# Sample attention of a decoder step: half of the page loads issued from GpSimd's queue

## What is computed

```
past = cache_kv_l[page_table].reshape(B, past_len, 4, N_KV, HEAD_DIM)     # B = 8, past_len = 2048
seq  = concatenate([past, rows, zeros])                                   # rows: the new tokens
kc, vc, ksb, vsb = branch_keys(seq, pe, w1, b1, w2)      # compressed keys; keys and values of blocks of 64
...
o_cmp = softmax(q kc) vc                                 # compressed branch; it also scores the blocks
kg, vg = ksb[top_k(score)], vsb[top_k(score)]            # 16 of 33 blocks of 64 tokens are selected
o_sel = softmax(q kg) vg
o_win = softmax(q kw) vw                                 # the last 512 tokens, from a window buffer
o = gates[0] * o_cmp + gates[1] * o_sel + gates[2] * o_win
```

## Time and profile before

| | |
|---|---|
| median of 3 runs | 1530.45 us (1529.3 to 1533.97) |
| the profiled execution | 1531.58 us, of which the span of the trace is 1529.9 us |
| mean granted TensorE clock | 0.992 of full speed |
| TensorE busy | 1434.4 us, 94% of the span |
| GpSimd busy | 480.1 us, 31% |
| sample attention loop | from about 1336 us to about 1512 us of the span |
| DMA moved in the whole span | 158.38 MB, mean 104 GB/s |

### The profile page before, as it was taken

How to read it: one execution, slowest core, us unless ns; L and a number is a source line. 1 busy time by engine, 2 the same in 40 slices (tenths; PEclk the granted TensorE clock), 3 DMA queues, 4 the chain that set the end, 5 groups by cost and what they waited for, 6 DMA issues and landing times.

```text
span 1529.9 us, 23043 instructions
## 1 busy us (share of the span) xinstructions
PE 1434.4 (94%) x8098; PEld 910.8 (60%) x8098; DVE 818.3 (53%) x1663; ACT 476.0 (31%) x1063; POOL 480.1 (31%) x449
## 2 busy tenths in 40 slices
PE   2999999999999999999999999999988889988886
PEld 2666666666666666777444444877755554455543
DVE  1578887888888888710112311132367774454443
ACT  1243343334434333222100000111355552064552
POOL 0855556566665555411100000000056562000000
PEclk9999999999999999999999999999999999999998
DMA  6543332333333312533510333114000004537870
GB/s 183 137 122 115 91 106 87 93 104 97 95 98 98 96 32 67 190 110 96 228 68 0 115 114 123 50 58 163 28 1 1 2 1 133 184 111 243 256 236 9
DMA packets 139549, 158.38 MB, mean 104 GB/s; under 512 B 16226, under 2 KB 103525, under 8 KB 139237
## 3 DMA queue, kind: packets, MB, share of 16 engines
q1 hardware_dynamic: 134162, 150.07, 31.5%
q10 hardware_dynamic: 5272, 6.83, 1.5%
HBM read 150.18 MB, written 16.38 MB: 109 GB/s over the span
## 4 chain that ended last, share of the span: by engine, by line
PE 84%; SPq 4%; DVE 3%; POOL 3%; issue 2%; ACTq 2%; DMA 2%; ACT 1%; DVEq 0%
PE bank L1354 25%; PE bank L1377 15%; PE bank L1531 8%; PE bank L1466 7%; PE bank L1493 5%; PE bank L1365 4%; PE bank L1693 4%; POOL arena L679 3%; PE bank L1639 2%; SPq L546 2%; PE bank L1670 2%; SPq L548 2%; PE bank L1654 2%; DMA arena<-in_cache_kv_dram 2%; DVE arena L1154 2%
## 5 line engine op out<-in xcount | busy, mean ns | idle before, releaser
L1014 DVE SCALAR_TENSOR_TENSOR arena<-arena 128x512 f32<-128x512 f32 x464 | 424.3, 988 | 0.0
L1354 PE MATMUL bank<-arena 128*128 128x288 f32 x1536 | 381.0, 408 | 0.9 <-DVE arena L981 0.9
L1354 PEld LDWEIGHTS bank<-arena 128*128 128x128 f32 x1536 | 292.0, 191 | 86.5 <-issue 8.3
L1377 PE MATMUL bank<-arena 128*128 128x508 f32 x512 | 239.8, 615 | 0.0
L1377 PEld LDWEIGHTS bank<-arena 128*128 128x128 f32 x512 | 93.3, 190 | 109.8 <-issue 109.8
L613 POOL TENSOR_TENSOR arena<-arena 128x248 f32<-128x248 f32 x128 | 134.1, 1082 | 1.3
L1531 PE MATMUL bank<-arena 128*128 128x288 f32 x512 | 127.0, 407 | 0.6 <-PE bank L1531 0.6
L398 DVE SCALAR_TENSOR_TENSOR arena<-arena,bank 128x512 f32<-128x512 f32 (+1 forms) x20 | 13.6, 680 | 209.8 <-PE bank L1466 160.8
L679 POOL TENSOR_SCALAR arena<-arena 128x128 f32<-128x128 f32 (+3 forms) x96 | 100.3, 1055 | 71.8 <-DVE arena L1162 71.8
L1531 PEld LDWEIGHTS bank<-arena 128*128 128x128 f32 x512 | 96.2, 190 | 27.3 <-issue 1.5
L1466 PE MATMUL bank<-arena 128*128 128x512 f32 x256 | 110.4, 592 | 0.0
(11 more groups left out here) (254 smaller groups left out, 1585.7 us busy)
## 6 DMA issues: line engine op xcount, KB each, us to landing
arena<-in_cache_kv_dram SPq DMA_DIRECT2D x256, 128.0 KB, 3.4
arena<-in_cache_kv_dram SPq DMA_DIRECT2D x128, 256.0 KB, 3.2
arena<-in_conv_w_in_dram SPq DMA_DIRECT2D x48, 512.0 KB, 4.2
arena<-in_nsa_w_in_dram SPq DMA_DIRECT2D x56, 256.0 KB, 4.7
arena<-in_conv_w_out_dram SPq DMA_DIRECT2D x16, 512.0 KB, 4.8
arena<-in_cache_win_dram SPq DMA_DIRECT2D x8, 1024.0 KB, 7.1
out_dram<-in_cache_win_dram SPq DMA_DIRECT2D x1, 8064.0 KB
arena<-in_x_prompt_dram SPq DMA_DIRECT2D x2, 2048.0 KB, 9.4
```

The costliest lines, as they stand in the source:

```text
L1014: ch.mark(dve.scalar_tensor_tensor(part, src, w, part, ALU.mult, ALU.add))
L1354: last = pe.matmul(bank[pair + h][:, 0:HALF], wi[:, n % WSLOT, k], xT[:, k, h * HALF:(h + 1) * HALF], start=k == 0, stop=k == KT - 1)
L1377: last = pe.matmul(out, wc[:, s, j, h * STEPS + k], x4[:, h, :, j:j + NC], start=(k == 0 and h == 0 and j == 0), stop=(k == STEPS - 1 and ...
```

## The change

The pages of buffers n = 2 and 3 are loaded from GpSimd's queue. SyncE keeps the windows and the buffers n = 0 and 1. The waits on `e_pv` and the completion semaphores are the same as before. GpSimd's new `load_pages` is the same function as SyncE's; for b = 0 its transfers stand ahead of the preparation of `vpair`, for b = 1 and later behind it.

```
+            def load_pages(b, n):
+                slot = (b % 2) * 4 + n
+                for i in range(4):
+                    pg = pool.value_load(pages[0:1, b * NPG + 4 * n + i:b * NPG + 4 * n + i + 1], min_val=0,
+                                         max_val=cache_kv.shape[1] - 1)
+                    pool.dma_start(kv[slot][:, i], cache_kv[0, bass.ds(pg, 1), :, 2:4].rearrange("o t s g d -> (o t) (s g d)")
+                                   ).then_inc(kv_in[slot], 16)
+
             pool.wait_ge(o_ev, KT)
+            for n in (2, 3):
+                load_pages(0, n)
             ch.link(pool.memset(vpair, 0.0))
             ch.link(pool.tensor_copy(vpair[0:64, :, HD:P], ...))
             pool.tensor_copy(vpair[64:128, :, 0:HD], ...).then_inc(staged, 1)
+            for n in (2, 3):
+                load_pages(1, n)
+            for b in range(2, NB):
+                for n in (2, 3):
+                    pool.wait_ge(e_pv, OUTS * (b - 2) + 3 + n)
+                    load_pages(b, n)
```

More of the change, by code:

```diff
@@ L558, in _ @@
             sp.dma_start(offs2, ln_b[1:2, :].broadcast_to([P, DM])).then_inc(s_ln, 16)
-            for n in range(4):
+            for n in range(2):
                 load_pages(0, n)
             load_window(1)
-            for n in range(4):
+            for n in range(2):
                 load_pages(1, n)
```

## The result

Slower: the median went from 1530.45 to 1541.66 us (1540.7 to 1545.52, five runs), a ratio of 1.0075 with a 95% interval of 1.0054 to 1.0096. I had said 1520.9.

What follows compares the result with a forecast made beforehand. The loop of freed buffer, SyncE's one-by-one page issue and landing was taken as the bound. A turn of 18.9 + 1.0 = 19.9 us against 21.51, six times, saves 9.6: from 1530.45 to 1520.9 us, range 1511 to 1545.

Steps and rivals of the forecast that it cites:

- What bounds the kernel: Sample attention loop: freed buffer, SyncE's page issues one after another, landing; better loading could give at most 21.7 us.
- SyncE's loop over eight pages: Sample attention loop: 11.8 us from buffer 0 freed to keys 2, 7.13 to weigh 2's end, 18.9 a turn.
- GpSimd's page: GpSimd's queue in the loop: register work 0.77 us plus issue 0.53 like a memset; its loop of 17.5 stays hidden.
- p: GpSimd's time per page in the loop, bounded between 0.77 and 2.63 us, taken as 1.30.
- Rival A: GpSimd's queue becomes the bound: each page costs it more than 1.87 us, slower, 1544 to 1562; chance 0.22.
- Rival C: VectorE keeps GpSimd from writing descriptors: 1.8 us a page, a turn of 21.0, time 1527; chance 0.06.
- The landing of GpSimd's pages: GpSimd's loop: 3.2 us from issue to landing; 0.4 more for its slower first byte would still be hidden.
- The two queues now overlap: GpSimd's pages beside SyncE's pages 5 to 8: SyncE's eighth lands 0.8 to 1.8 us later, 1.0 taken, 19.9 a turn.
- Rival B: The DMA engines are the bound: eighth page late by 2.0 to 2.6 us, time 1527 to 1530, no change; chance 0.13.
- The clock adds about 2 either way: TensorE after a 2 us wait at keys 2: a stretch at the lower clock may follow, or none; about 2 us.
- No cost ahead of the loop: Before the loop: GpSimd's first 8 pages take at most 21 us ahead of vpair, first read some 80 later.
- windows for nothing: Windows go out after weigh 0, 4.6 us before buffer 0 frees, landing in 7.3 with 10.5 to spare: no cost.

Runs made afterwards that it cites:

- Numbers ahead, on one queue: Kernel before, SyncE reading the page numbers of buffers 0 and 1 before waiting for buffer 0, issuing all sixteen pages: 1512.93 us, ratio 0.9891.
- half the bytes: Page loads bring only the keys, 128 KB of 256: changed kernel 1515.02 us, ratio 0.9899; kernel before 1520.95 us, ratio 0.9941.
- the last experiment: Changed kernel with SyncE's page numbers read ahead, plus the window issued after weigh 1 instead of weigh 0: 1510.53 us, ratio 0.9869.
- GpSimd held back: Changed kernel, GpSimd starting on a sequence's pages only when SyncE has issued its eight, from b = 2 on: 1543.27 us, ratio 1.01.
- the kernel with numbers ahead: Changed kernel, both queues, SyncE reading its eight page numbers before it waits for buffer 0: 1525.9 us, ratio 0.9981.
- swapped buffers: Changed kernel with the buffers exchanged, GpSimd loading 0 and 1, SyncE 2 and 3: 1552.41 us, ratio 1.0132.
- The filler: Changed kernel with 24 spare TensorE transposes ahead of the wait at keys 2, from b = 2 on: 1534.9 us, ratio 1.0031.
- buffers dealt in turn: Changed kernel with GpSimd loading buffers 1 and 3, SyncE 0 and 2: 1535.35 us, ratio 1.0029.

## Why the prediction was wrong

**What bounds the kernel: right.** The loop over freed buffer, issues and landing sets the turn. Numbers ahead, on one queue, and half the bytes both shortened it and the turn followed; with the waits nearly gone, the last experiment came to 17.99 us.

**SyncE's loop over eight pages: right as a term.** 11.8 us from freeing to keys 2 without the overlap was measured as 11.8 to 12.1 with GpSimd held back.

**GpSimd's page: right in kind, and cheaper.** p is 1.16 us, I took 1.30. Rival A is out: its eighth page of b = 4 was there at 1422.93 + 3.5 = 1426.4, and keys 4 came at 1432.60. Rival C is out too: the pages follow each other by 1.15 to 1.17 us whatever VectorE does, but for one gap of 1.45 in b = 3 and one in b = 6, which stand at the same pages in the shorter turns of the kernel with numbers ahead. The Trainium skill (SBUF — State Buffer, SBUF: two separate sides) names fast copies within SBUF as what locks GpSimd out of writing descriptors; VectorE's frequent copies here come from PSUM, and the even intervals agree.

**The landing of GpSimd's pages: right where they are alone.** A first page of buffer 0, with nothing beside it, lands in 2.9 to 3.3 us from GpSimd's queue (swapped buffers, mean of six 3.1) and in 2.4 to 2.9 from SyncE's (changed kernel, mean 2.6). The Trainium skill (DMA: Bandwidth & Descriptors, Latency and other measured facts) has about 0.4 us between the first bytes of the two kinds of queue, and by these landings, 0.45 apart, the trace agrees.

**The step that failed: "The two queues now overlap ... I take 1.0".** I gave this delay 0.8 to 1.8 us. The six turns have 15.01, 14.44, 14.76, 15.45, 13.68 and 14.74 us from weigh 2 to keys 2, mean 14.68: a delay of 14.68 - 11.8 = 2.9. In b = 4 it is the landing of the eighth page, 6.0 against 3.2. I had sized it by sharing out the highest rates of the trace, 405 or 336 GB/s, over four pages. But the engines moved 213 to 277 GB/s from 1415 to 1420, while the pages piled up, and the high rate came only from 1420 on. (The 336 wasn't even the second highest: the kernel before has 398 GB/s from 1430 to 1432. A right reading would have made the delay smaller still.) A warning was in the rows: the earlier trace rows has a share of 0.80 at 255 GB/s, with one queue asking for 236. I read the missing 0.2 as room. Over six turns the error is (14.68 - 12.8) x 6 = 11.3 us. Rival B named this mechanism and the sign that came ("pages land more than 5 us after their issue"), and priced it up to 2.6 us, 1530; by itself, at 2.9, it would have been 1532. The wide range of 1511 to 1545 takes in 1541.66 only because it was stretched for rival A, whose mechanism didn't occur: that is luck.

**The second step: "The clock adds about 2 either way".** From keys 2 to keys 4 the sum had 7.13 us, with nothing for the clock, and it was 8.45 in the mean: (8.45 - 7.13) x 6 = 7.9 us. Before, the same stretch without its waits had been over 7.13 by 3.4 us in all six turns, most of it in b = 3. The change merged several waits of about 1 us into one of about 4, and behind five of the six long ones the granted clock was 0.50. I looked for such stretches in the trace of before, found one after a wait of 1.9 us, and didn't ask how the length of the waits would change. The filler gave 6.8 us back.

The two make 19.2 us, and 1520.9 + 19.2 = 1540.1 is what was measured within 1.6. The loss against before closes as well: 22.5 - 17.6 = 4.9 us more of waits and 7.9 - 3.4 = 4.5 more between keys 2 and keys 4 without them, of 9.8.

**No cost ahead of the loop, and windows for nothing: right for this change.** Windows landed in 5.3 us in the median. That they would be in the way as soon as the rest is quick, I had not seen.

**The rule I set aside.** The Trainium skill (DMA: Bandwidth & Descriptors, Issuing engines are not separate DMA queues) says that all queues end on the same 16 engines and save only issue time. The half-bytes pair agrees with the first. I used it for the 1.0 us and took the gain in issue time as secure. Numbers ahead on one queue shows that the issue time was there to save (1529.57 - 1512.93 = 16.6 us), but not by running two queues into each other.

**What stays open.** Why the engines move only 213 to 277 GB/s at a share of 0.73 to 0.88 from 1415 to 1420 while over 370 follow at once. The swapped buffers exclude a fixed preference for one queue, and the row of the filler kernel (404 GB/s with TensorE, VectorE and ScalarE busy) excludes that a busy TensorE alone keeps the rate down; nothing run here tells whether the place of the pages in memory or the issue itself is behind it. Open as well is why the buffers dealt in turn, with the pages of keys 2 no longer last in a queue, gained so little. Also open is why a lead of only 0.17 to 0.65 us is enough for the window to hold back a page by 3 us.

## What to carry to other kernels

Ask not how many queues issue, but when the last transfer that the next wait needs goes out, and what is in flight beside it; a second queue that starts before that one has landed can make it late (here by 2.9 us a turn). The first thing to move is work that needs no wait (here the reading of the page numbers) out of the path from freed buffer to issue, and the second is to hold back what isn't due. And count the length of each wait of TensorE, not only their sum: here one of about 4 us left 1.4 to 1.6 us of slow work behind it in five turns of six, and the waits before the change, 0.15 to 2.5 us at a time, left 0.2 to 0.4 a turn, but for one turn with 1.9.

## What the runs showed of the hardware

- GpSimd issues a 256 KB page DMA with a number read from memory every 1.16 us (0.54 us of it the DMA instruction), nearly as fast as SyncE (1.11), and with VectorE busy beside it.
- Landing of a 256 KB page: the first of a burst, alone, 2.4 to 2.9 us from SyncE (changed kernel) and 2.9 to 3.3 from GpSimd (swapped buffers); the eighth, with pages of the other queue beside it, 5.0 to 6.1 from SyncE and 6.0 to 7.0 from GpSimd; 7.0 with a 1 MB transfer issued just ahead on the other queue (numbers ahead).
- SyncE, with the page numbers read ahead, issues eight pages in about 5 us (0.6 each), and with no other queue its own pages then land in 2.9 to 5.5 us.
- The DMA engines moved 404 GB/s in a microsecond in which TensorE, VectorE and ScalarE were busy (filler kernel, 1421 to 1422).
- Granted clock: after waits of 3.5 to 4.5 us in all five cases at 0.50 for some 3 us (8.6 to 8.75 us for a stretch of 7.13), after one of 2.75 not at all (7.18), after one of 2.63 in the filler kernel again (8.70); with the buffers dealt in turn, after 2.76 again and after 2.83 not. So the length of the wait alone doesn't decide it.
